# Four gate products per layer by seven products, reordered waits, and unread products ahead of the experts

## The reference, cut to what matters

```python
# each of the two layers of the first block
proj = x @ w_in                                   # 1024 -> 6144; the last 3072 are the gates
g = sigmoid(gates).reshape(bn, s, 3, 1024)
merged = g[:, :, 0] * (br_a @ w_a) + g[:, :, 1] * (br_b @ w_b) + g[:, :, 2] * (br_c @ w_c)
x = layer_norm(DN_ALPHA * x + merged @ w_out, ln1_g, ln1_b)
x = layer_norm(DN_ALPHA * x + (silu(x @ w1) * (x @ w3)) @ w2, ln2_g, ln2_b)
# the second block, after its mixer
x = layernorm(ALPHA * x + g1 * (mixed @ w_out), ln1_g, ln1_b)
h = modulate(x, sh2, sc2)
ffn = sum over the 2 chosen experts e of weight * ((silu(h @ ex_gate[e]) * (h @ ex_up[e])) @ ex_down[e])
x = layernorm(ALPHA * x + g2 * ffn, ln2_g, ln2_b)
```

## Time and profile before

| what | value |
|---|---|
| three executions | 2031.52, 2032.51, 2032.98 us |
| profiled execution: its time | 2031.6 us |
| its span in the trace | 2029.9 us |
| first block, first layer | 0 to 500 us |
| first block, second layer | 500 to 989 us |
| second block up to its router | 989 to 1545 us |
| router, plan and first expert | 1545 to 1605 us |
| loop over 14 pairs | 1605 to 2018 us, 29.4 us each |
| last norm and output | 2018 to 2030 us |
| busy PE, DVE, ACT, POOL | 97%, 54%, 23%, 12% of the span |

### The profile page before, as it was taken

The page is one execution under the profiler, slowest core; times in us unless marked ns, Lnnn a source line. Parts: engine busy times, 40 slices in busy tenths (PEclk is TensorE's granted clock), DMA queues, the critical chain, the costliest instruction groups (busy, mean ns, idle before and its releaser), DMA issues.

```text
span 2029.9 us, 35655 instructions
## 1 busy us (share of the span) xinstructions
PE 1970.1 (97%) x14679; PEld 1371.6 (68%) x14679; DVE 1093.5 (54%) x1846; ACT 475.6 (23%) x908; POOL 251.4 (12%) x234
## 2 busy tenths in 40 slices
PE   8999999999999999999999999999998999999997
PEld 5778869974768877995445565899985444444443
DVE  2685276654569247665668846545447333233324
ACT  3165110000426311000231134433323101101111
POOL 4684000000568100000000002000000000000000
PEclk9999999999999999999999999899997899999999
DMA  8333545544533254545822234200011999999994
GB/s 254 125 125 104 191 140 167 166 168 150 186 125 125 104 207 141 172 133 202 311 83 70 96 125 146 105 3 3 4 47 75 378 427 424 428 424 429 427 429 177
DMA packets 138851, 385.51 MB, mean 190 GB/s; under 512 B 16951, under 2 KB 64415, under 8 KB 127585
## 3 DMA queue, kind: packets, MB, share of 16 engines
q1 hardware_dynamic: 138721, 383.61, 50.5%
HBM read 382.54 MB, written 1.05 MB: 189 GB/s over the span
## 4 chain that ended last, share of the span: by engine, by line
PE 91%; ACT 4%; DVE 3%; issue 2%; DMA 0%; ACTq 0%; DVEq 0%; SPq 0%
PE psum L408 17%; PE psum L666 12%; PE psum L1609 10%; PE psum L3186 9%; PE psum L2353 8%; PE psum L3211 5%; PE psum L709 5%; PE psum L3118 3%; PE psum L426 3%; PE psum L3243 2%; PE psum L725 2%; PE psum L629 2%; PE psum L642 1%; PE psum L2769 1%; PE psum L1814 1%
## 5 line engine op out<-in xcount | busy, mean ns | idle before, releaser
L408 PE MATMUL psum<-arena,ring 128*128 128x256 f32 x1728 | 382.5, 380 | 1.0 <-ACT arena L776 1.0
L408 PEld LDWEIGHTS psum<-arena,ring 128*128 128x128 f32 x1728 | 324.5, 189 | 55.0 <-issue 8.2
L2353 PE MATMUL psum<-arena 64*64 64x64 f32 (+1 forms) x4320 | 179.8, 238 | 2.6 <-issue 1.5
L2353 PEld LDWEIGHTS psum<-arena 64*64 64x64 f32 x4320 | 171.6, 134 | 4.6 <-issue 2.7
L666 PE MATMUL psum<-arena,ring 128*128 128x128 f32 x1280 | 149.5, 275 | 0.6 <-issue 0.6
L666 PEld LDWEIGHTS psum<-arena,ring 128*128 128x128 f32 x1280 | 146.1, 192 | 0.8 <-issue 0.8
L1609 PE MATMUL psum<-arena,ring 128*128 128x512 f32 (+2 forms) x432 | 142.0, 490 | 0.0
L776 ACT ACTIVATE arena<-psum 128x512 f32<-128x512 f32 (+2 forms) x84 | 44.6, 557 | 381.4 <-PE psum L408 163.4
L1609 PEld LDWEIGHTS psum<-arena,ring 128*128 128x128 f32 (+1 forms) x432 | 81.2, 188 | 60.6 <-issue 55.3
L666 PE MATMUL psum<-arena 128*128 128x128 f32 x960 | 113.7, 275 | 0.0
L666 PEld LDWEIGHTS psum<-arena 128*128 128x128 f32 x960 | 110.4, 192 | 0.0
(11 more groups left out here) (480 smaller groups left out, 2998.2 us busy)
## 6 DMA issues: line engine op xcount, KB each, us to landing
ring<-in_w_in_dram SPq DMA_DIRECT2D x29, 2048.0 KB, 8.1
ring<-in_ffn_w_dram SPq DMA_DIRECT2D x46, 1024.0 KB, 7.8
arena<-in_ex_gate_dram SPq DMA_DIRECT2D x15, 2048.0 KB, 12.0
arena<-in_ex_up_dram SPq DMA_DIRECT2D x15, 2048.0 KB, 16.4
arena<-in_ex_down_dram SPq DMA_DIRECT2D x15, 2048.0 KB, 16.7
ring<-in_ex_gate_dram SPq DMA_DIRECT2D x14, 2048.0 KB, 9.1
ring<-in_ex_up_dram SPq DMA_DIRECT2D x14, 2048.0 KB, 13.5
ring<-in_ex_down_dram SPq DMA_DIRECT2D x14, 2048.0 KB, 15.2
```

The lines of the kernel that those rows point to most:

```text
L408: ins = pe.matmul(bank[:, j, :], w[:, kc, c * P:(c + 1) * P], moving[:, kc, :], start=kc == 0, stop=kc == k - 1)
L2353: ins = pe.matmul(bank[r, u, :], a[r, u], b[r, u], start=i == 0, stop=i == len(terms) - 1)
```

## The change

Gate groups 8 to 11 leave the head loop as plain products. Their 1024 columns are two units of `w_in` (10 and 11), and each is made by seven products with DVE's sums: PE's `gates_by_seven(u)` (keys `gp`), DVE's `gate_token_sums` once and `gate_weight_sums(u)` twice a layer, DVE's `gate_blocks(u)` to add up the blocks, and ACT's `sigmoids(u)` over a whole unit. The products of branch a move from behind the loop into heads 5 and 6 (`BRANCH_WITH`), with their `w_a` loaded ahead of the last two `w_in` units.

Other parts: tile 1 of x is turned within the first product and not between the two; tile 1 of x1 is turned ahead of the last quarter of `up(0)`'s first pass; `attend_out(3)` moves between the two glu products, and ACT's copy of it with it; DVE's order around `w_out`'s sums changes, and PE no longer waits there for its own last branch product before it frees the parameters (DVE does that now). `lif` waits for each pair of turned chunks and not for all. `unread_products` makes PE multiply the identity by a row tile into a bank that is overwritten later: 4 ahead of the turning of token tile 0 and 3 ahead of tile 1, 1 ahead of the router's products of tile 1, 3 ahead of the second route and 3 ahead of the first gather, each of 128x128 by 512 columns. The first gather uses two banks, so its products can follow by halves. In the loop, ACT copies the hidden units before the gather. One unread square root is made at the start of `finish_scalar`.

```diff
 def layer_units():
-    units = [("w_in", c) for c in W_IN_ORDER]
-    units += [("w_a", 0), ("glu_w", 0), ("w_c", 0), ("w_b", 0), ("w_out", 0), ("w_out", 1)]
+    units = [("w_in", c) for c in W_IN_ORDER[:-2]] + [("w_a", 0)] + [("w_in", c) for c in W_IN_ORDER[-2:]]
+    units += [("glu_w", 0), ("w_c", 0), ("w_b", 0), ("w_out", 0), ("w_out", 1)]
...
-GATES_WITH = [[0], [1, 2], [3], [4, 5], [6], [7, 8], [9], [10, 11]]
+GATES_WITH = [[0], [1, 2], [3], [4, 5], [6], [7], [], []]
+BRANCH_WITH = [[]] * 5 + [[0, 2], [1, 3], []]
...
+                    if first and kc == DC - 2:
+                        turn_tile("x_in", "xT", 1)
...
+        def gates_by_seven(u, halves=range(2)):
+            w = K.weights(("w_in", 10 + u), DC, BANK)
+            b = lambda i, j: w[:, 4 * i:4 * i + 4, j * T:(j + 1) * T]
...
+            banks = [[(b(0, 0), a11)], [(b(1, 0), a12), (b(1, 1), s4)], [(t2, s2), (b(0, 1), s1)], [(t3, s3), (t4, a22)]]
+            for half in halves:
+                if half == 0:
+                    pe.wait_ge(K.landed(("w_in", 10 + u)), K.landed_count(("w_in", 10 + u), l))
+                    pe.wait_ge(K.sem["sums"], K.count("sums", l, turn_of_sums(("gx", 0))))
+                else:
+                    pe.wait_ge(K.sem["sums"], K.count("sums", l, turn_of_sums(("gt", u))))
+                for i in (2 * half, 2 * half + 1):
...
+                    for x, (weights, moving) in enumerate(banks[i]):
+                        for j in range(2):
+                            for k in range(4):
+                                ins = pe.matmul(bank[:, x, j, :], weights[:, k, j * P:(j + 1) * P], moving[:, k, :],
+                                                start=k == 0, stop=k == 3)
...
-        for i in range(2):
-            channels(("glu",), i, w, K.y_g, k=WC)
+        channels(("glu",), 0, w, K.y_g, k=WC)
         attend_out(HEADS // 2 - 1)
+        channels(("glu",), 1, w, K.y_g, k=WC)
...
-        pe.wait_ge(K.full(("br", 1, 3)), K.full_count(("br", 1, 3), l))
-        pe.sem_inc(K.sem["params_free"], 1)
...
-                elif n >= 5:
-                    pe.wait_ge(K.sem["sums"], K.count("sums", l, turn_of_sums(("wo", n - 4))))
+                elif n == 3:
+                    pe.wait_ge(K.sem["sums"], K.count("sums", l, turn_of_sums(("wo", 3))))
...
+            up(0, slice(tt * P, (tt + 1) * P), first=tt == 0, last=tt == 1,
+               between=(lambda: turn_tile("x1", "x1T", 1)) if tt == 0 else None)
...
+        def gate_weight_sums(u):
+            dve.wait_ge(K.landed(("w_in", 10 + u)), K.landed_count(("w_in", 10 + u), l))
+            if u:
+                dve.wait_ge(K.full(("gp", u - 1, 3)), K.full_count(("gp", u - 1, 3), l))
...
+            tt_op(t3, b22, b12, ALU.subtract).then_inc(link.sem, 1)
...
+            tt_op(b12, b12, b11, ALU.subtract).then_inc(link.sem, 1)
...
+            tt_op(t2, b22, b12, ALU.subtract).then_inc(link.sem, 1)
...
+            tt_op(t4, b21, t2, ALU.subtract).then_inc(K.sem["sums"], 1)
...
-    for s in range(2):
-        for q in range(4):
-            pe.wait_ge(K.empty(("hT", s, q)), K.drained_count(("hT", s, q)))
...
+    for kc in range(DC):
+        if kc % 2 == 0:
+            for s in range(2):
+                pe.wait_ge(K.empty(("hT", s, kc // 2)), K.drained_count(("hT", s, kc // 2)))
+        ins = pe.matmul(K.bank(("lif", 0)), K.gate_w[:, kc, :], K.hsT[:, kc, :], start=kc == 0, stop=kc == DC - 1)
...
+def unread_products(pe, K, key, n):
+    pe.wait_ge(K.sem["dma_ln3"], K.count("dma_ln3"))
+    pe.wait_ge(K.empty(key), K.empty_count(key))
+    for _ in range(n):
+        pe.matmul(K.bank(key), K.ident, K.ln2_rows[:, 0, 0:BANK], start=True, stop=True)
...
     def token_tile_turned(tt):
+        unread_products(pe, K, ("h2T", 2 * tt), 4 - tt)
...
+        if tt == 1:
+            unread_products(pe, K, ("rt", tt), 1)
...
+    unread_products(pe, K, ("h2", 0, 0), 3)
     pe.wait_ge(K.sem["route"], K.count("route", 0, 2))
...
 def pair_tensor(pe, K):
+    unread_products(pe, K, ("first", 1), 3)
...
         silu(0)
         silu(1)
-        gathered(0)
         hidden_turned(0)
         hidden_turned(1)
+        gathered(0)
...
+    act.activation(sums[:, 3:4], K.ln_eps, ACT.Sqrt)
```

More of the change, by code:

```diff
@@ L83, in layer_groups @@
             keys += states(n + AHEAD)
-        keys += [("gate", g) for g in GATES_WITH[n]]
+        keys += [("gate", g) for g in GATES_WITH[n]] + [("br", 0, i) for i in BRANCH_WITH[n]]
+        keys += [("gp", 0, i) for i in range(4)] if n == HEADS - 1 else []
         if n > 0:
@@ L89, in layer_groups @@
             keys += [("y", n // 2)]
-    keys += [("br", 0, i) for i in range(4)] + [("pT", HEADS - 1)]
-    keys += [("glu", i) for i in range(2)] + [("o", HEADS // 2 - 1)]
+    keys += [("gp", 1, i) for i in range(4)] + [("pT", HEADS - 1)]
+    keys += [("glu", 0), ("o", HEADS // 2 - 1), ("glu", 1)]
     for x in (2, 1):
@@ L577, in layer_tensor @@
                 gates(g)
+            if n == 5:
+                for i in range(2):
+                    pe.wait_ge(K.empty(("mix", i)), K.drained_count(("mix", i), l))
+            if BRANCH_WITH[n]:
+                branch(0, "w_a", BRANCH_WITH[n])
+            if n == HEADS - 1:
+                gates_by_seven(0)
             if n > 0:
@@ L583, in layer_tensor @@
                 state_outputs(n // 2)
[L585 to L589, removed]
-        for i in range(2):
-            pe.wait_ge(K.empty(("mix", i)), K.drained_count(("mix", i), l))
-        branch(0, "w_a")
+        gates_by_seven(1)
         attend_values(HEADS - 1)
@@ L632, in layer_tensor, with up @@
         out_by_seven()
-        def up(c, tokens=slice(0, T), first=True, last=True):
+        def up(c, tokens=slice(0, T), first=True, last=True, between=None):
             both = K.weights(("w13", c), 2 * DC, FFN_COLS)
@@ L640, in up @@
                 for j in range(2):
+                    if between and (i, j) == (1, 1):
+                        between()
                     for kc in range(DC):
@@ L674, in layer_tensor @@
             turned("x1T", tt)
-            up(0, slice(tt * P, (tt + 1) * P), first=tt == 0, last=tt == 1)
+            up(0, slice(tt * P, (tt + 1) * P), first=tt == 0, last=tt == 1,
+               between=(lambda: turn_tile("x1", "x1T", 1)) if tt == 0 else None)
         for c in range(1, FFN_UNITS):
@@ L833, in attended, with first_product, sigmoids @@
             drain(("o", hp), K.oT[:, hp, :], src=lambda bank: bank[:, 0:T])
+        def first_product(u):
+            drain(("gp", u, 0), K.gp1[:, u], src=lambda bank: bank[:, 0:T])
+        def sigmoids(u):
+            act.wait_ge(K.empty(("gp", u, 3)), K.drained_count(("gp", u, 3), l))
+            unit = K.gates[:, 16 + 4 * u:20 + 4 * u, :]
+            act.activation(unit, unit, ACT.Sigmoid).then_inc(K.sem["gated"], 1)
         for n in range(HEADS):
@@ new lines, in gate_token_sums @@
+        def gate_token_sums():
+            a11, a12, a21, a22 = (K.xT[:, 4 * k:4 * k + 4, tt * P:(tt + 1) * P] for tt in range(TT) for k in range(2))
+            s1, s2, s3, s4 = K.gx_sums
+            tt_op(s1, a21, a22, ALU.add).then_inc(link.sem, 1)
+            dve.wait_ge(link.sem, link.count())
+            tt_op(s2, s1, a11, ALU.subtract).then_inc(link.sem, 1)
+            dve.wait_ge(link.sem, link.count())
+            tt_op(s4, a12, s2, ALU.subtract)
+            tt_op(s3, a11, a21, ALU.subtract).then_inc(K.sem["sums"], 1)
@@ L1164, in layer_vector @@
             gated(2, i)
-        for i in range(3):
+        for i in range(2):
             gated(1, i)
```

158 lines of the change are left out of this document (111 added, 47 removed).

## The result

The changed kernel took 2008.09 us (median of four: 2006.20, 2007.12, 2009.07, 2009.56) against 2032.74 us for the kernel before in the same session; the ratio is 0.9874, with an interval of 0.9862 to 0.9887. The forecast was 2010.4 us. The profiled execution took 2009.56 us with a span of 2007.8 us, so against the profiled execution of before (span 2029.9) it is 22.1 us shorter. That is the sum in the prediction to the tenth, but not with the same terms, as the stages show.

What follows compares the result with a forecast made beforehand. PE, busy 97% of the span, was taken as the bound. Terms of 14.5 + 1.3 + 6.3 = 22.1 us off 2031.6 gave 2009.5, forecast as 2010.4 since that execution lay 0.9 under the median; eight-in-ten range 2006 to 2018.

Steps and rivals of the forecast that it cites:

- Gates 8 to 11: Gate units in both layers: seven products of 12.5 us replace 14.06 us a unit, saving 6.2 us if DVE's sums keep up.
- The rival that the sums are late: Gate part: weight sums take 2.28 us each, four 9.1 against 5.4, so 3.7 us a layer lost, 2017.8 us; chance 0.12.
- Waits in the layers: Both layers: 1.9 us from waits for the attention copy and PE's last branch product, 1.9 from `w_out`'s sums.
- Turned tiles: Tile 1 turned inside the product hides copies: 1.5 us at `up(0)`, 1.2 us at the first product, both layers together.
- `lif`: Starts after the first of four chunk-pair copies, not the last, where it waited 2.0 us: 1.85 us saved.
- The end: End of the span: the unread square root moves a 1.28 us table load into idle time, saving 1.3 us.
- Ahead of the experts and the loop: Unread products holding the clock give 5.6 us, ACT's copy order 4.2; of 9.8 together, 6.3 us counts.
- the cap: Loop transfers at 427 GB/s leave weights 5.3 us ahead, plus 1.0, so PE can gain only 6.3 us.
- unread products late: Ahead of the experts: groups run at the lower clock, delaying route and loop transfers up to 4.8 us; 2012.5 to 2017.3; chance 0.20.
- the prediction's signs of being wrong: Gate-product waits over 0.5 us, clock 0.5 at first gather, later first-pair transfers, or 29.1 us passes without weight waits.
- The rival of a clock that falls in the loop: PE stops for weights each pass, the clock falls, 14 x 5.1 = 71 us lost, about 2082 us; chance 0.02.
- the weights keep up: Loop: 427 GB/s is PE's pace, not the transfers' own, so all 9.8 us count: 2006.9 us; chance 0.12.

Runs made afterwards that it cites:

- the fifth weight sum: Changed kernel with the first of unit 11's four weight sums made twice, 1.26 us more of VectorE per layer: 2008.52 us.
- the later profile: Changed kernel run once more, unaltered, beside the kernel with smaller groups: 2006.56 us (2005.14 to 2007.81), ratio 0.9869.
- the three runs with smaller groups: Changed kernel without the three unread products ahead of the second route: 2007.07 us; with also two, not three, ahead of tile 1: 2005.00, then timed at 2005.83.
- the one with the eighth product: Changed kernel with an eighth block product, the first made twice, in each of the four gate units: 2015.72 us.

## Why the prediction was right

**Gates 8 to 11** (forecast 6.2). The two units take 12.70 + 12.51 us in place of 28.12: 2.9 a layer, 5.8 in both. The slack of about 0.4 us, PE's bound and the price of a block product were each tested and stand. The rival that the sums are late is out: four end after 5.0 us (212.09 to 217.09), as worked out.

**Waits in the layers** (1.9 + 1.9). Of the 5.37 us that heads to `w_out` lost undisturbed, 2.9 are the gates' and 2.5 the waits', so 4.9 in both layers and not 3.8. The step that fell short is the pricing of a wait at its idle row: the idle rows have 4.0 us for six waits, and with the 0.25 us that the fifth weight sum showed for each they become 5.5; the 4.9 lie between. That these waits make up all of the 2.5 us is a difference and was not tested by itself; PE's idle rows in the second layer's stretch went from 2.15 to 0.21 us. The choice of 1.9 and not 2.1 for `w_out`'s sums was too cautious as well, since that wait is gone whole.

**Turned tiles** (1.5 + 1.2). `up(0)` gave 1.06 and 1.83 us. The first is the wait of 0.83 and 0.23 more. The second has another 0.77, most of it a wait of 0.60 us at L666 in the profile of before that the forecast did not look at; in the kernel before with the loop's order, whose layers are the same, it was 0.25 us, so it varies. The second layer's first product gave 0.88 for a wait of 0.84, and not 0.4: no wait is left there, so the tile was ready in time after all. The first layer's took 1.24 us less, more than its wait of 0.83; start-up varies by more than that, so the rest is chance.

**`lif`** (1.85): the wait fell from 2.0 to 0.5 us, 1.5. The stage around it can't tell, since it holds clock falls of different length (746.6 to 749.0 in the changed kernel's variants).

**The end** (1.3): 1.26, and 1.28 alone in the kernel before. Of the further drain of about 1380 ns that the Trainium skill ("ScalarE: Activation LUTs", What ACT_TABLE_LOAD costs) adds to the load, this case shows nothing: by it the end would have been 2.66 us shorter.

**Ahead of the experts and the loop** (6.3, of 9.8 without the cap): 6.68 in this profile. The cap was the right idea, and the half-loaded down matrices give what it cost: without it 472.40 - 463.67 = 8.7 us. The row that "never passes 427" was that of one pass; 1650 to 1700 us of the kernel before had 429, which changes the cap little. So the uncapped 9.8 was 1.1 too high, and the cap took 2.0 and not 3.5. That 6.3 and 6.7 lie so close is in part luck, since two errors cancel: from SP's first issue to the last row put back it was 435.8 us before and 427.9 after, so there were 7.9 us to win and not 5.3 + 1.0, but that issue came 1.2 us later after the mixer, where the prediction put the route neither earlier nor later. Inside it, the way to the loop gave 4.1 us and not 5.6: the group ahead of the second route ran at 1.2 GHz, was 1.9 us late, and put the plan off. That is the rival "unread products late", at one of the two places that it named, though the clock was up at the gather in this profile. Two of the prediction's signs of being wrong are there: the later first issue, and passes of 29.10 us with no wait for weights, six of them here and all in the later profile, where the gather had the lower clock too. The loop's order gave 0.25 us a pass and not 0.30.

The rival of a clock that falls in the loop is out: of the eleven profiles with the changed layers only the one without unread products has a fall there, once, at the loop's start, though PE waits for weights in the late passes of five. Nor did the change do less than it says: the turning lies inside the product and the table load in idle time.

The cap has a simpler form than slack and gap. From SP's first issue for the loop to the last row put back, the changed kernel took 427.9 us, the three runs with smaller groups 428.2, 428.3 and 427.9, the one with the eighth product 428.1; runs that loaded as much and never waited for weights took longer, 429.0 and more. So the end comes at the later of two times: the first issue plus 428 us, or the loop's first product plus 407.5 us. The changed kernel's second profile is 21.5 us from issue to first product and is PE's; its first has 18.3 and is the transfers'. The rival "the weights keep up" therefore holds in some executions and not in others, and is worth about 1 us, not 3.5. Both numbers are read from these profiles; the half-loaded down matrices show that the loads set the first, and no run moved the first issue alone.

**The clock in the first layer** was in no term: 3.21 us lost in this profile, 1.56 in the later one, none in eight of the eleven profiles of kernels with the changed layers. How far falls and start-up together explain the spread of the executions is not shown: of the first four the two near 2009 had a mean clock of 0.990 and 0.991 and the other two 0.994, but of the later four the two near 2005 had 0.992 and those near 2008 had 0.994. Without the fall of this profile the span would have been 25.3 us shorter and not 22.1. The forecast was thus right in its mechanisms, and by luck closer in its total than its terms deserved: the layers' terms, about 3 us too low (12.7 against 15.8, with start-up's share in it), stood against a clock fall of 3.2 us that it did not foresee.

## What to carry to other kernels

On a PE-bound path price a wait at its idle row, and expect up to a quarter of a microsecond more: `up(0)` gave 1.06 and 1.07 us for 0.83 and the late sum cost 1.00 for 0.74, but the second layer's first product gave 0.82 for 0.79 and the hidden copies 0.25 for 0.26. When the profile shows transfers busy all the time behind PE, write down both ends, first issue plus their time and first product plus PE's, before adding gains up: the later one counts. Unread products gained 5.4 us here in all, though they did not keep the clock up in every execution; ahead of a step that others plan by, they run at whatever clock there is, and must be sized for the lower one.

## What the runs showed of the hardware

- The clock can fall with PE busy all the time: 105 to 112 us, at 1.2 GHz, PE 7.00 of 7.00 us. Such falls came in pieces of 3.4, 6.8, 10.2, 13.7 and 27.3 us. They moved with start-up: the four profiles of a kernel with the changed layers whose first product ended by 26.31 us include three with a fall at 105 us (the fourth is the one without unread products, at 25.66), and those that ended later have none there. One had it at 587 us, the same place in the second layer. Why is not shown.
- A fall of 6.8 us costs about half of that when PE's products fill it: 3.21 us at 105 us.
- A transfer rate of 434 GB/s stood over 6.8 us in the run without unread products, once at 1.2 GHz (1586.3 to 1593.1) and once at 2.4 GHz (1606.7 to 1613.5), so these rows show no part of PE's clock in it; whole passes had 427 to 429.

```profile
1606.70:1613.50 6.80, 6.79 (x35) 2.56 (x35) 1.38 (x2) 1.43 (x4) 0.00 (x0) 1.00 1.01 434
```

- The Trainium skill ("DMA: Bandwidth & Descriptors", Where 436 GB/s comes from) has 435 as the ceiling of the ports and about 358 as the limit of a core's HBM, which it says binds for loads from HBM. These loads ran above the second in every pass; the first is met for a moment (434) and not held over a pass (427 to 429), so the row was the one to plan by.
